# Attention by pairs of heads with a distance table per head, squares of X on ScalarE, and the fourth weight unit split ahead, in a two-block transformer kernel on one core

## The reference, cut to what matters

```python
s = jnp.einsum('brnqhe,brnkhe->brnhqk', qb, kk) * (HEAD_DIM ** -0.5)
bias = -slopes[:, None, None] * dist[None]           # slopes = 2 ** -(h + 1)
s = jnp.where(valid[None, None, :, None], s + bias, -jnp.inf)
m = jnp.max(s, axis=-1, keepdims=True)
p = jnp.exp(s - m)
denom = jnp.sum(p, axis=-1, keepdims=True)
...
for window, dilation in DILATED_BRANCHES:            # (128, 1), (512, 4), (2048, 16)
    o, l = dilated_window_branch(q, k, v, slopes, window, dilation)
...
w = jax.nn.softmax(jnp.stack(lses, axis=-1), axis=-1)
o = jnp.einsum('bshn,nbshe->bshe', w, jnp.stack(outs, axis=0))
```

## Time and profile before

| | |
|---|---|
| median of 3 runs | 2990.05 us (2989.93 to 2990.61) |
| the profiled execution | 2988.9 us, span 2987.1 us |
| TensorE busy | 2929.6 us, 98% of the span |
| VectorE, ScalarE, GpSimd busy | 1327.0, 1002.0, 392.8 us |
| granted TensorE clock, mean | 0.995 |
| read from HBM | 255.03 MB |

### The profile page before, as it was taken

The page is one execution under the profiler, slowest core; times in us unless marked ns, Lnnn a source line. Parts: engine busy times, 40 slices in busy tenths (PEclk is TensorE's granted clock), DMA queues, the critical chain, the costliest instruction groups (busy, mean ns, idle before and its releaser), DMA issues.

```text
span 2987.1 us, 32386 instructions
## 1 busy us (share of the span) xinstructions
PE 2929.6 (98%) x13550; PEld 2412.1 (81%) x13550; DVE 1327.0 (44%) x1783; ACT 1002.0 (34%) x1345; POOL 392.8 (13%) x424
## 2 busy tenths in 40 slices
PE   8999989999999999999999999999999999999998
PEld 7888877577888888888887888888888888788887
DVE  5553267645433343324656433244332465643324
ACT  4232234453323232323424423234222342443222
POOL 3110056402110000010131000100001014200010
PEclk9999999999999999999999999999999999999999
DMA  3332212122332232322212232222322221123322
GB/s 137 99 99 94 97 57 71 24 71 85 99 99 95 89 99 93 98 93 84 84 50 71 92 99 97 94 85 92 99 99 92 85 78 57 64 99 99 96 95 78
DMA packets 76017, 260.40 MB, mean 87 GB/s; under 512 B 11728, under 2 KB 11856, under 8 KB 75856
## 3 DMA queue, kind: packets, MB, share of 16 engines
q1 hardware_dynamic: 75872, 258.34, 26.6%
HBM read 255.03 MB, written 2.10 MB: 86 GB/s over the span
## 4 chain that ended last, share of the span: by engine, by line
PE 91%; DVE 6%; ACT 1%; issue 1%; SPq 0%; DMA 0%; POOL 0%; DVEq 0%; ACTq 0%
PE bank L325 25%; PE bank L327 25%; PE bank L326 25%; PE bank L341 2%; PE bank L347 2%; PE bank L342 2%; PE bank L692 2%; PE bank L444 1%; DVE Hl L1302 1%; PE bank L455 1%; PE bank L381 1%; PE bank L377 1%; PE bank L378 1%; DVE Hl L1300 1%; DVE wlo L1294 1%
## 5 line engine op out<-in xcount | busy, mean ns | idle before, releaser
L1294 DVE TENSOR_TENSOR wlo<-wraw,whi 128x1024 fp32r<-128x1024 f32 x474 | 588.7, 1254 | 823.6 <-ACT whi L803 823.0
L325 PE MATMUL bank<-Hh,whi 128*128 128x512 f32 x2320 | 909.3, 392 | 18.1 <-DVE wlo L1294 12.1
L327 PE MATMUL bank<-Hl,whi 128*128 128x512 f32 x2320 | 904.1, 390 | 0.0
L326 PE MATMUL bank<-Hh,wlo 128*128 128x512 f32 x2320 | 903.6, 389 | 0.0
L803 ACT ACTIVATE whi<-wraw 128x1024 fp32r<-128x1024 f32 x479 | 498.9, 1055 | 946.5 <-DMA wraw<-weights 946.0
L325 PEld LDWEIGHTS bank<-Hh,whi 128*128 128x128 f32 x2320 | 436.2, 188 | 115.8 <-issue 19.9
L327 PEld LDWEIGHTS bank<-Hl,whi 128*128 128x128 f32 x2320 | 435.9, 188 | 91.6
L326 PEld LDWEIGHTS bank<-Hh,wlo 128*128 128x128 f32 x2320 | 436.2, 188 | 88.8
L325 PE MATMUL bank<-Ah,whi 128*128 128x512 f32 x1056 | 411.8, 390 | 0.0
L327 PE MATMUL bank<-Al,whi 128*128 128x512 f32 x1056 | 410.9, 389 | 0.0
L326 PE MATMUL bank<-Ah,wlo 128*128 128x512 f32 x1056 | 410.8, 389 | 0.0
(11 more groups left out here) (259 smaller groups left out, 2469.6 us busy)
## 6 DMA issues: line engine op xcount, KB each, us to landing
wraw<-weights SPq DMA_DIRECT2D x479, 512.0 KB, 3.5
X<-x_t SPq DMA_DIRECT2D x8, 256.0 KB, 6.7
y_t<-X SPq DMA_DIRECT2D x8, 256.0 KB, 2.0
Y<-masks SPq DMA_DIRECT2D x1, 512.0 KB, 8.8
MUb<-ssm SPq DMA_DIRECT2D x1, 256.0 KB, 8.2
tmp<-ssm SPq DMA_DIRECT2D x1, 256.0 KB, 4.0
zsum<-attention SPq DMA_DIRECT2D x1, 256.0 KB, 4.1
MUb<-attention SPq DMA_DIRECT2D x1, 256.0 KB, 4.2
```

Source lines behind the costliest of these rows:

```text
L325: pe.matmul(b, sh, mh, start=start, stop=False)
L326: pe.matmul(b, sl, mh, start=False, stop=False)
L327: signal(pe.matmul(b, sh, ml, start=False, stop=stop), keys)
L1294: dve.tensor_tensor(wlo[:, u % NS, :], wraw[:, u % NS, :], f32(whi[:, u % NS, :]), SUB).then_inc(*S.done("weights_lo", ("lo", u)))
```

## The change

It has six parts.

1. **Pairs of heads.** Units are ordered (2hp, tb), (2hp + 1, tb). One step d of the loop takes a double unit: on TensorE two `turn`, two `scores` (of d + 2), and `values(d - 1)`. `values` now multiplies per (pair, tb): 2 * (tb + 1) matmuls of 128 columns, alternating between the heads. Six score buffers (tmp 0 to 3, acc, sq). ScalarE copies PT of the odd units, VectorE of the even.
2. **One table per head** holds log(count) - slope * distance. L1736 becomes a plain add of bank and table, L1746 is gone, and ScalarE's exp sums by itself (`accum_out`). SyncE loads eight tables of 256 KB rather than two; from the fifth on it waits for scores that free their tiles.
3. **s5_out** is no longer beside attention: after attention come `half_rows`, then ssm, gelu's transposes and glu. `lags` stand two by two at d = 6 to 9.
4. **Squares of X** for k = 1 to 6 on ScalarE into tmp, added into acc by VectorE (`add_before`), at f1, m1 and f2; GpSimd's `pre_norm` is gone.
5. **The fourth unit** of each stage is split after Hh of k = 4 (ScalarE) and after Hl of k = 4 (VectorE); in f1, where three are loaded ahead, unit 2.
6. **FIRST = 4:** for k = 1 to 3 `gemm_group` multiplies all four tiles with Hh before it waits for Hl.

```diff
-    units = [(h, tb) for h in range(HEADS) for tb in range(4)]
+    units = [(2 * hp + e, tb) for hp in range(HEADS // 2) for tb in range(4) for e in range(2)]
+    score = tmp[0:4] + [acc, sq]
...
-                if fresh:
+                last = k == KD - 1
+                if fresh and k < FIRST:
                     pe.wait_ge(*S.at(("Hh", fresh, k)))
+                    for i in range(4):
+                        hi, lo, ends = tiles[i] = tile()
+                        pe.matmul(bs[i][:, :], hi, Hh[:, k, :], start=False, stop=False)
+                        pe.matmul(bs[i][:, :], lo, Hh[:, k, :], start=False, stop=False)
                     pe.wait_ge(*S.at(("Hl", fresh, k)))
...
+                pe.wait_ge(*S.at(("PT", 2 * d)))
+                pe.wait_ge(*S.at(("PT", 2 * d + 1)))
+                for sb in range(tb + 1):
+                    for e in range(2):
+                        h = 2 * hp + e
+                        ins = pe.matmul(b[64 * e:64 * e + 64, tb * P:(tb + 1) * P], Vt[:, sb, 64 * h:64 * h + 64],
+                                        PT[:, (2 * d + e) % 4, sb * P:(sb + 1) * P], start=tb == 0, stop=sb == tb,
+                                        skip_group_check=True)
...
+                for d in range(-2, 16):
+                    if d >= 0:
+                        turn(2 * d)
+                        turn(2 * d + 1)
+                    if d + 2 < 16:
+                        scores(2 * d + 4)
+                        scores(2 * d + 5)
+                    if d > 0:
+                        values(d - 1)
+                    yield d
+                values(15)
...
+            gemm_group("qk1", None, (("H free", "m1"),), lambda k: next(heads))
+            for d in heads:
+                if d < 10:
+                    lags(2 * d - 12)
+                    lags(2 * d - 11)
+            half_rows("m1o", ("Hh", "m1o"), ("Hl", "m1o"))
+            for _ in s5_out():
                 pass
-            half_rows("m1o", ("Hh", "m1o"), ("Hl", "m1o"))
...
+            elif k < KD - 1:
+                if k > 4:
+                    act.wait_ge(*S.at(("acc add", st, k - 4)))
+                act.activation(tmp[k % 4][:, :], X[:, k, :], ACT.Square).then_inc(
+                    *S.done("squares", ("square in", st, k)))
...
+                if k == 4:
+                    hi_to(START[then] + 8)
...
+                            act.activation(s, s, ACT.Exp, bias=rcol[:, o:o + 1],
+                                           accum_out=rcol[:, o + 1:o + 2]).then_inc(
+                                *S.done("probabilities", ("exp", u)))
...
+        def add_before(st, k):
+            if 0 < k < KD - 1:
+                dve.wait_ge(*S.at(("square in", st, k)))
+                dve.wait_ge(*S.at(("acc add", st, k - 1) if k > 1 else ("acc 0", st)))
+                keys = (("acc add", st, k),) + ((("acc", st),) if k == KD - 2 else ())
+                dve.tensor_tensor(acc[:, :], tmp[k % 4][:, :], acc[:, :], ADD).then_inc(*S.done("sums", *keys))
...
                 if k:
                     rest(k - 1)
+                    if k == 5:
+                        lo_to(START[then] + 8)
+                    if pre_g:
+                        add_before(then, k - 2)
             rest(KD - 1)
+            if pre_g:
+                add_before(then, KD - 2)
...
-                dve.scalar_tensor_tensor(s[:, 0:n], Dp[:, T - n:T], -2.0 ** -(h + 1), bank(("scores", u))[:, 0:n], MUL,
-                                         ADD).then_inc(*S.done("scores", ("score", u), empties=[("scores", u)]))
+                dve.tensor_tensor(s[:, 0:n], bank(("scores", u))[:, 0:n], dist[h % 4][:, T - n:T], ADD).then_inc(
+                    *S.done("scores", ("score", u), empties=[("scores", u)]))
...
-                dve.scalar_tensor_tensor(s[:, 0:n], s[:, 0:n], 1.0, Cn[:, T - n:T], MUL, MUL,
-                                         accum_out=rcol[:, o + 1:o + 2]).then_inc(*S.done("scores", ("sum", u)))
-                dve.wait_ge(*S.at(("sum", u)))
...
             if k == 1:
                 lo(1)
+            if k == 5:
+                lo(2)
+            add_before("f1", k - 1)
...
+            if u == att_at + 2:
+                sp.wait_ge(*S.at(("score", 6)))
+                distances(4)
+                sp.wait_ge(*S.at(("score", 7)))
+                distances(5)
             if u == skip_at:
+                sp.wait_ge(*S.at(("score", 14)))
+                distances(6)
+                sp.wait_ge(*S.at(("score", 15)))
+                distances(7)
                 sp.wait_ge(*S.at("lags"))
```

## The result

The changed kernel takes 2964.14 us in the median of four runs (2961.35 to 2964.73), against 2990.33 (2989.93 to 2993.08) in the same comparison: ratio 0.9909, 95% interval 0.9891 to 0.9926. The profiled execution took 2964.73, where the prediction's sum said 2964.3.

A forecast was written before the change was run, and what follows sets the result against it. TensorE, busy for nearly all of the 2987.1 us span, was taken as the bound. Terms of -7.5 + 1.3 - 3.4 - 8.4 - 6.6 = -24.6 gave 2964.3 profiled and a median forecast of 2965; range 2956 to 2976.

The forecast's parts named there:

- The sum: Whole kernel: the terms together give -24.6 us, 2964.3 for the profiled time.
- Start of f1: First group of f1: k = 4 starts 5.8 us earlier and half clock behind the wait goes, -7.5 us.
- Start of m1: First group of m1: the wait for wlo becomes one before colr, with half clock on spread and fillers, +1.3 us.
- if colr's wait is short: Sign in m1 that the prediction is wrong; it expected TensorE to wait 8 to 11 us for colr.
- f2: First group of f2: no GpSimd work there, fourth unit split earlier, k = 6 starts 3.4 us earlier, -3.4 us.
- The six starts: First groups of a0, h0, b0, a1, h1, b1: FIRST gives -3.0 us, the fourth unit -5.4, together -8.4.
- Attention beside qk1: Attention while qk1 runs: 37.9 us instead of 46.4, with values and scores each at half cost by overlapping array halves.
- Attention after qk1: From the end of the qk1 group at 524.1 to half rows: 45.8 us, with TensorE waiting for VectorE and ScalarE.
- End of m1: Half rows, ssm, gelu, glu: glu's first row ends 10.55 us after ssm; -8.6, +2 for half clock, net -6.6.
- m1's wait really goes: Rival in m1: colr comes up to 6 us earlier without half clock, -8 us on the sum, 2957; chance 0.12.
- Nothing overlaps in TensorE: Rival in attention: pairs cost their full columns, +4.5 us beside qk1, nothing behind it, 2970; chance 0.15.
- Half clock for longer: Rival behind qk1: half clock through half rows and ssm, +10 us, 2975; chance 0.12.

The follow-up runs named there:

- colr_sooner: The full change, with VectorE making the reciprocal and colr behind the third part of Wri/Wt instead of the fifth: 2957.78 us, ratio 0.9890.
- scores_apart: The full change, with a unit's transposes put between the two score matmuls of a pair: 2974.15 us, ratio 0.9947.
- half_rows_last: The full change, with half rows behind gelu's transposes and the recurrence's states copied ahead of attention's last step: 2957.09 us, ratio 0.9892.
- starts_alone: Parts 4 to 6 alone on the kernel before, with attention, tables and the end of m1 as before: 2971.81 us, ratio 0.9935.
- all_three: The full change with colr earlier, half rows behind gelu's transposes and splits spread out, without the 12 fillers ahead of ssm: 2945.13 us, ratio 0.9850.
- unit_as_before: The full change with part 5 undone, the fourth unit split where it was: 2976.55 us, ratio 0.9955.
- gpsimd_squares: The full change with part 4 undone, squares and their sum back on GpSimd: 2971.35 us, ratio 0.9933.
- kf_sooner: all_three, with VectorE scaling Qf and Kf of the third and fourth head blocks at steps 5 and 6: 2942.92 us, ratio 0.9836.
- first_1: The full change with part 6 undone, FIRST = 1: 2968.03 us, ratio 0.9925.
- values_apart: The full change, with one head's values matmuls all before the other's within a double unit: 2964.60 us, ratio 0.9916.

## Why the prediction held, step by step

**The sum** (-24.6 for -24.15 in the profiles) is closer than its terms, and that is luck: attention gave 1.75 less than written, m1's start 0.5 and f2 0.3 less; the six starts gave 1.1 more, the stretches costed at nothing 0.8, f1 0.2. Added again from what it states, the prediction's sums come out to within 0.1.

**Start of f1**: right, -7.66 for -7.5, and by its steps. GpSimd's squares were 4.1 of it and the place of unit 2 was 2.2 (each undone alone); the other 1.4 can go only when both are undone.

**Start of m1**: right in place and sum (+1.56 for +1.3), wrong in its inside. The wait for wlo turned into one for colr, as said, but of 5.3 and not 8 to 11: by the prediction's own sign ("if colr's wait is short") this step was off. colr came 1.5 earlier against the shift of the stage, not 0.3 to 0.9; and TensorE reached it later, because half clock fell into u already (401.3) and again behind the wait (414.9). Undoing part 5 puts 8.2 of wait back without moving v, which shows that the wait of 6.6 in the earlier trace rows was never worth its length.

**f2**: -3.07 for -3.4. "No GpSimd work there" is wrong of the kernel before, where GpSimd's squares run beside the Hl from 667.6 to 684.6 and an Hl takes 1.5. With the squares on GpSimd f2 gains only 0.9; with the fourth unit as before it gains nothing (+0.3). So it takes both parts, where the prediction gave all to the fourth unit. The sum was near because its steps of 2.05 + 0.65 are those of the change.

**The six starts**: -9.54 for -8.4. The term of FIRST was under-sized: 0.5 was written, 0.57 to 0.67 measured (3.8 in all). The fourth unit gave 1.9 in b0, a1 and h1 for 1.8 (with FIRST = 1). There FIRST pays only with it: with the unit as before, b0 and a1 gained nothing.

**Attention beside qk1**: predicted to end at 524.1 on the clock of before, measured 517.65 + 5.84 = 523.5. Two errors go against each other. Scores overlap wholly, not by half, which is 2.15 better than written; values less than wholly, 0.85 worse: each product pays some 0.16 beside its columns (four records in two halves take 0.37, sixteen 1.02), so that the five took 3.2 instead of 2.35. The other 0.7 between these two and the 0.6 that the end came early is not explained. The overhead of each matmul that was weighed against the change by the Trainium skill, "TensorEngine Tiling (Array Packing)", Instruction Overhead, did not show as an addition to its columns: within a half, records of 128 columns start 0.107 apart, a quarter of the 0.43 for 512.

**Attention after qk1**: the step that failed, though not by enough to upset the sum. "45.8 us" to half rows was 49.7. The term of the waits was mis-sized: "3.8 because at d = 9 VectorE waits behind ScalarE's lags and two Hh" was 3.4 and right, but the 3.2 at d = 13, where the third pair's bank is held until VectorE's Hl, was not seen, and half clock was counted once (+2) and stood there in three stretches, 17.1 us. Spreading the splits takes 7.4 off the stretch, more than the two waits together. So all that the change gains in attention lies beside qk1, whose matmuls start within 35.3 us instead of 42.0; from its last matmul to f2's first the change takes 138.9 us, the kernel before 137.1.

**End of m1**: glu's first row ended at 606.57, 10.7 after ssm, for 10.55. It showed as one wait of 1.65 rather than 5 in four pieces, because half clock stretched the matmuls into the gaps. Half rows first was a loss within the change: put last, with the states' copies ahead, 7.0 come back in the median (7.8 in the stretch).

**The rivals.** "m1's wait really goes" did not happen, but colr_sooner makes it happen and pays 7.0, near the 8 written. "Nothing overlaps in TensorE" is refuted by scores_apart. "Half clock for longer" was partly there: 17 us of it behind qk1 and 6.8 in glu's first row, but hardly any in half rows and none in ssm, where the rival had it. The prediction counted three stretches at half clock before; the trace has a fourth, of 3.4 us at 1625.9. SyncE's new waits held up nothing that shows: no wait of TensorE names a DMA.

## What to carry to other kernels

A wait's length is not its price. Ask what the waiting engine needs next and when that is there: 8.2 us for wlo cost nothing, since colr was no sooner, while 5.3 for colr cost 7.0, with the half clock behind it. Where a loop is bound by the chain over several engines, put work that only looks ahead (splits for a later stage) off the steps on which a bank or a reciprocal hangs, and keep a block of dense matmuls (half rows) to lay over a chain of ScalarE such as gelu. When an edit's stretch shows no gain, a better median alone does not make it one; and compare the half clock of two profiles before a difference of 1 to 3 us is put down to an edit.

## What the runs showed of the hardware

**Half clock that no edit explains.** In the second block, which the attention edits don't touch, the 14 profiles have none to two stretches of 3.4 us at half clock each. They stand at few places, always at a wait of TensorE. Two such places are the waits of 1.60 us for Sg at the fillers (L452), two in every profile: of these 28, 11 have one (after at 1558.4, half_rows_last at 1550.2 and 2512.7), 17 pass without. A third is a wait of 1.2 to 1.45 for acc ahead of b0 (before at 1625.9, starts_alone at 1618.1, all_three at 1591.3). One stands behind the wait of 2.27 for wlo in h1 of unit_as_before. colr_sooner, gpsimd_squares and kf_sooner have none. At the first three places each moves what follows by 1.4 to 1.7 us, set against kf_sooner; of the one at 1558.4 only 0.8 is left soon after, since waits for Hl take up the rest. Why one run falls and another not is open.

The first block has it too. Between v and f2 five kernels have the same instructions on TensorE, and took 231.8 (unit_as_before), 232.5 (first_1), 233.8 (after and colr_sooner) and 234.9 us (gpsimd_squares), with 17.1 to 23.9 us at half clock. Such a spread, of some 2 to 3 us on a profile, is why sums were compared by stretch, and it lies on every figure of a stretch in m1 above.

**TensorE overlaps halves beyond direct neighbours.** With one head's eight records in front of the other's, the second head's first record started 0.006 us behind the first head's fifth, and the two ran beside each other until the first head's were through (values_apart, as read above).

**Scores' length in time is that of one.** Two fp32 matmuls on SBUF rows 0 to 63 and 64 to 127, into two banks, started 0.006 to 0.007 us apart and took 1.06 together.
